# Routed experts in a two-layer trunk: expert rows summed in PSUM instead of stored and gathered, and slot rows read one block ahead on another queue

## The reference

```python
def moe_ffn(h, router_w, router_bias, w_gate, w_up, w_down):
    ...
    scores = jax.nn.sigmoid((t @ router_w).astype(jnp.float32))
    sel = scores + router_bias.astype(jnp.float32)
    ...                       # the best of 4 groups of experts, and in it the best 2 experts
    wsel = jnp.take_along_axis(scores, eidx, axis=-1)
    wsel = wsel / wsel.sum(-1, keepdims=True)
    comb = jnp.sum(jax.nn.one_hot(eidx, N_EXPERTS, dtype=jnp.float32) * wsel[..., None], axis=1)
    hg = jnp.einsum('td,edf->tef', t, w_gate)
    hu = jnp.einsum('td,edf->tef', t, w_up)
    act = jax.nn.silu(hg) * hu * comb[:, :, None].astype(t.dtype)
    return jnp.einsum('tef,efd->td', act, w_down).reshape(B, L, D)

# in trunk, for each layer:
        y = moe_ffn(h, ...)
        x = layer_norm(ALPHA * x + g2 * y, P['ln_w'][l, 1], P['ln_b'][l, 1])
```

## Time and profile before

| what | value |
|---|---|
| median of 3 runs | 1208.53 us |
| profiled execution | 1201.09 us |
| its span, and TensorE's mean granted clock | 1199.4 us, 0.951 |
| TensorE busy in the span | 1013.1 us (84%) |
| SyncE's queue q1 | 291.40 MB, 62.9% of 16 engines |
| POOL's queue q0 | 41.78 MB, 10.2% |
| ScalarE's queue q10 | 10.49 MB, 2.5% |

### The profile page before, as it was taken

One profiled execution on the slowest core, in us unless ns is written; L12 is line 12 of the kernel. 1 busy time (PEld: TensorE's weight loads), 2 busy tenths in 40 slices (PEclk: granted clock), 3 DMA queues, 4 the chain that ended last, 5 costly groups with the idle time before them and its releaser, 6 DMA issues.

```text
span 1199.4 us, 24149 instructions
## 1 busy us (share of the span) xinstructions
PE 1013.1 (84%) x9499; PEld 561.7 (47%) x9499; DVE 400.3 (33%) x1149; ACT 239.8 (20%) x507; POOL 190.9 (16%) x389
## 2 busy tenths in 40 slices
PE   4899998899769899795679999999978977998564
PEld 2344447654435455453345555455454544555231
DVE  0320115744612222121353533645552221222116
ACT  0401003631411121111131111210141121121102
POOL 0320000300032222122110001002004221222111
PEclk9999999899789999898889999999979998999988
DMA  8998232977589999999892314636765799899984
GB/s 354 324 343 299 95 126 97 350 298 317 222 302 396 388 407 393 397 399 394 305 377 99 140 71 143 243 123 241 292 256 211 270 391 408 337 395 393 394 349 158
DMA packets 76278, 344.62 MB, mean 287 GB/s; under 512 B 8883, under 2 KB 9011, under 8 KB 62900
## 3 DMA queue, kind: packets, MB, share of 16 engines
q1 hardware_dynamic: 54756, 291.40, 62.9%
q0 software_dynamic: 14512, 41.78, 10.2%
q10 hardware_dynamic: 6944, 10.49, 2.5%
HBM read 320.02 MB, written 23.63 MB: 287 GB/s over the span
## 4 chain that ended last, share of the span: by engine, by line
PE 63%; DMA 21%; DVE 10%; ACT 2%; issue 2%; SPq 1%; POOL 0%; POOLq 0%; ACTq 0%; DVEq 0%
PE bank L954 13%; PE bank L743 12%; PE bank L1019 11%; PE bank L961 7%; DMA ring<-in_moe_w_up_dram 7%; PE bank L872 7%; DMA ring<-in_ada_w_dram 3%; DMA ring<-in_moe_w_down_dram 3%; DMA arena<-in_moe_w_up_dram 3%; PE bank L633 3%; DMA ring<-in_ev_w_in_dram 3%; PE bank L1122 1%; PE bank L1098 1%; ACT arena L1409 1%; DVE arena L1531 1%
## 5 line engine op out<-in xcount | busy, mean ns | idle before, releaser
L954 PE MATMUL bank<-ring,arena 128*32 128x256 f32 x2496 | 149.9, 391 | 28.8 <-DMA ring<-in_moe_w_up_dram 25.7
L743 PE MATMUL bank<-ring,arena 128*128 128x512 f32 x336 | 146.7, 598 | 2.5 <-DMA ring<-in_ev_w_in_dram 2.5
L954 PE MATMUL bank<-arena 128*32 128x256 f32 x1792 | 108.1, 395 | 28.3 <-DMA arena<-in_moe_w_up_dram 28.3
L1019 PE MATMUL bank<-arena,ring 128*128 128x384 f32 x384 | 126.3, 492 | 1.9 <-issue 1.9
L1529 DVE TENSOR_TENSOR arena<-arena,bank 128x64 f32<-128x64 f32 x136 | 27.4, 201 | 296.2 <-ACT arena L1409 296.2
L954 PEld LDWEIGHTS bank<-ring,arena 128*32 128x32 f32 x2496 | 83.7, 113 | 88.5 <-issue 41.7
L961 PE MATMUL bank<-ring,arena 128*32 128x256 f32 x1440 | 87.0, 382 | 27.3 <-DVE arena L1531 22.2
L743 PEld LDWEIGHTS bank<-ring,arena 128*128 128x128 f32 x336 | 64.2, 192 | 82.9 <-issue 80.2
L1019 PEld LDWEIGHTS bank<-arena,ring 128*128 128x128 f32 x384 | 73.5, 192 | 54.4 <-issue 5.0
L954 PEld LDWEIGHTS bank<-arena 128*32 128x32 f32 x1792 | 60.3, 114 | 72.0 <-issue 39.4
L872 PE MATMUL bank<-ring,arena 128*128 128x512 f32 x192 | 83.2, 593 | 1.3 <-DVE arena L2096 1.3
(11 more groups left out here) (367 smaller groups left out, 1074.9 us busy)
## 6 DMA issues: line engine op xcount, KB each, us to landing
ring<-in_ada_w_dram SPq DMA_DIRECT2D x24, 2048.0 KB, 13.4
ring<-in_moe_w_down_dram SPq DMA_DIRECT2D x20, 2048.0 KB, 23.5
ring<-in_moe_w_gate_dram SPq DMA_DIRECT2D x18, 2048.0 KB, 24.1
ring<-in_moe_w_up_dram SPq DMA_DIRECT2D x18, 2048.0 KB, 29.4
arena<-in_moe_w_gate_dram SPq DMA_DIRECT2D x14, 2048.0 KB, 26.7
arena<-in_moe_w_up_dram SPq DMA_DIRECT2D x14, 2048.0 KB, 31.9
arena<-in_moe_w_down_dram SPq DMA_DIRECT2D x12, 2048.0 KB, 20.1
ring<-in_ev_w_in_dram SPq DMA_DIRECT2D x7, 2048.0 KB, 19.4
```

Source lines behind the costliest of these rows:

```text
L743: last = pe.matmul(bank[3 * (c % 2) + t], hT[:, k, t * P:(t + 1) * P], slot8(n)[:, k, :], start=k == 0, stop=k == KT - 1)
L954: last = pe.matmul(bank[1][q * BLK:(q + 1) * BLK, 0:HALF], slot_inT[:, k, :], both[:, :, k, q * P:(q + 1) * P], start=k == 0, stop=k == KT ...
L1019: last = pe.matmul(bank[c % 3][:, 0:T], slot8(n)[:, k, (c % 4) * P:(c % 4 + 1) * P], hT[:, k, :], start=k == 0, stop=k == KT - 1)
```

## The change

Expert results are no longer stored to DRAM and gathered. Six of the eight PSUM banks (`joined`) hold the sum for all 384 tokens over a whole expert stage. For each block VectorE builds a matrix `sel_w` that holds a token's routing weight where the token's slot lies in the block, and zero elsewhere; TensorE multiplies it with the block's result, 12 matmuls per block (`add_to_tokens`), each with 32 rows. They stand between gate and up of the next block and its down, and a last one behind the stage. In return the transposes on TensorE go (VectorE transposes the rows in blocks of 32), as do the gathers and the joins. Gate, up and down use banks 0 and 1 only.

The rows of a block are read by one DMA of 128 KB from ScalarE's queue into one buffer `slot_ahead`, in ScalarE's loop behind `row_rdy`; block 2's rows by SyncE. POOL only copies them. TensorE picks block 0 directly as channels by rows. The routing weights and slots of all tokens are spread to all partitions at the start of a stage (`along_tokens`). Behind layer 0 some column work is moved behind the first norms.

```diff
+        psum = ctx.enter_context(nc.psum_tensor("psum", [P, 8 * 512], F32))
+        bank = [psum[:, i * 512:(i + 1) * 512] for i in range(8)]
+
+        joined = psum[:, 2 * 512:8 * 512].rearrange("p (q t c) -> p t q c", q=4, t=NT)
...
-        slot_in = at(19456, 512, rows=2 * BLK)
+        slot_in = at(19456, 2 * P)
+        slot_ahead = at(19712, 2 * P)
         slot_inT = at(19968, KT, BLK)
         silu_g = at(20224, FT, BLK)
         act_rows = at(20352, FT, BLK)
         act_T = at(4096, FT, BLK)
-        slot_out = [at(4224, 512, rows=2 * BLK), at(6400, 512, rows=2 * BLK)]
-        slot_ahead = [at(5376, 512, rows=2 * BLK), at(5888, 512, rows=2 * BLK)]
+        slot_out = at(4224, HALF)
+        sel_w, sel_w1 = at(4736, T), at(5120, T)
+        token_slot, token_w = at(5632, 2, T), at(6400, 2, T)
         SPARE = 7168
-        picked = at(8192, NT, 2, D)
+        norm_scratch = at(8192, D)
...
+        def rows_in(queue, layer, block):
+            queue.dma_start(slot_ahead, slots[bass.ds(block * BLK, BLK), :].rearrange("s (g c) -> g s c", g=4)).then_inc(MS[layer]["row_in"], 16)
...
             blocks = pool.value_load(table[0:1, NE:NE + 1], min_val=NE, max_val=MAX_BLOCKS)
-            pool.wait_ge(trips_rdy, l + 1)
...
-
             before_last = pool.value_load(table[0:1, NE - 1:NE], min_val=NE - 1, max_val=MAX_BLOCKS)
-            pool.wait_ge(S["down_mm"], before_last)
-            pool.tensor_tensor(idle, wsel[:, 0, 0:1], wsel[:, 0, 0:1], ALU.add).then_inc(pool_chain, 1)
-            pool.wait_ge(pool_chain, 2 * l + 2)
+            with pool.Fori(2, blocks + 2) as b:
+                pool.wait_ge(S["row_in"], b * 16 - 16)
+                pool.wait_ge(S["rowT"], b)
+                pool.tensor_tensor(idle, eps_col, eps_col, ALU.add)
+                pool.tensor_copy(by_k(slot_in), slot_ahead.rearrange("p (s k) -> p k s", k=KT)).then_inc(S["row_rdy"], 1)
+
             if l == 0:
+                pool.wait_ge(S["row_rdy"], blocks + 1)
+                pool.wait_ge(S["down_mm"], before_last)
+                pool.tensor_tensor(idle, eps_col, eps_col, ALU.add).then_inc(pool_chain, 1)
+                pool.wait_ge(pool_chain, 2)
                 norm_gate_rows(pool)
-            for odd in range(2):
...
-                                            bass.IndirectOffsetOnAxis(ap=idx[:, r * NT + t:r * NT + t + 1], axis=0)).then_inc(gathered[t], 16)
+            pool.wait_ge(S["row_in"], blocks * 16 + 16)
+            pool.tensor_tensor(rows_over[:, l:l + 1], eps_col, eps_col, ALU.add)
...
-            for c in range(WARM):
-                pe.matmul(bank[3], ident, h_tok[:, c % NT, 0:512], start=True, stop=True)
-            rows_due = counter(pe, f"rows_due{l}", 1)
+
+            def along_tokens(b, column):
+                for t in range(NT):
+                    last = pe.matmul(b[:, t * P:(t + 1) * P], column(t).to_broadcast([P, P]), ident, start=True, stop=True)
+                return last
+
+            def begin_sums(b):
+                pe.matmul(b, tri[:, 0:1].to_broadcast([P, P]), keep[:, 0:512], start=True, stop=False)
+
+            pe.wait_ge(weights_rdy, l + 1)
+            for r in range(2):
+                last = along_tokens(bank[1 + r], lambda t: wsel[:, r, t:t + 1])
+            last.then_inc(spread_mm, 1)
+            for b in bank[3:]:
+                begin_sums(b)
+            pe.wait_ge(idx_rdy, l + 1)
+            pe.wait_ge(spread_act, 2 * l + 1)
+            for r, b in ((0, bank[1]), (1, bank[2])):
+                last = along_tokens(b, lambda t: slot_f[:, r * NT + t:r * NT + t + 1])
+            last.then_inc(spread_mm, 1)
             pe.wait_ge(table_rdy, l + 1)
             begin_of = EXPERT_ORDER + [NE]
             begin, end, after = 0, *[pe.value_load(table[0:1, begin_of[i]:begin_of[i] + 1], min_val=i, max_val=MAX_BLOCKS) for i in (1, 2)]
             pe.wait_ge(pick_rdy, l + 1)
+            for k in range(KT):
+                for t in range(NT):
+                    last = pe.matmul(bank[0][:, k * BLK:(k + 1) * BLK], h_tok[:, t, :].rearrange("p (c k) -> p k c", k=KT)[:, k, :],
+                                     pick[:, t, 0:BLK], start=t == 0, stop=t == NT - 1)
+            last.then_inc(pick_mm, 1)
+            pe.wait_ge(spread_act, 2 * l + 2)
             for t in range(NT):
-                for q in range(4):
-                    block, h = divmod(q, 2)
-                    last = pe.matmul(bank[2][q * BLK:(q + 1) * BLK, :], pick[:, t, block * BLK:(block + 1) * BLK],
-                                     h_tok[:, t, h * 512:(h + 1) * 512], start=t == 0, stop=t == NT - 1)
+                for g in range(4):
+                    last = pe.matmul(bank[1][g * BLK:(g + 1) * BLK, HALF:2 * HALF], pick[:, t, BLK:2 * BLK],
+                                     h_tok[:, t, g * HALF:(g + 1) * HALF], start=t == 0, stop=t == NT - 1)
             last.then_inc(pick_mm, 1)
-
...
-                last.then_inc(S["rowT_mm"], 1)
+            begin_sums(bank[2])
 
             def gate_and_up(s, k):
 
                 both = pair_of(s)
                 for q in range(4):
-                    last = pe.matmul(bank[1][q * BLK:(q + 1) * BLK, 0:HALF], slot_inT[:, k, :],
+                    last = pe.matmul(bank[0][q * BLK:(q + 1) * BLK, 0:HALF], slot_inT[:, k, :],
                                      both[:, :, k, q * P:(q + 1) * P], start=k == 0, stop=k == KT - 1)
                 return last
 
             def down(s, f):
 
-                for tile, q in enumerate((0, 2, 1, 3)):
-                    last = pe.matmul(bank[5][tile * BLK:(tile + 1) * BLK, 0:HALF], act_T[:, f, :],
+                for q in range(4):
+                    last = pe.matmul(bank[1][q * BLK:(q + 1) * BLK, 0:HALF], act_T[:, f, :],
                                      slot4(s + 2)[:, f, q * HALF:(q + 1) * HALF], start=f == 0, stop=f == FT - 1)
                 return last
 
+            def add_to_tokens(turn, closing=False):
+
+                for t in range(NT):
+                    if t == 2:
+                        pe.wait_ge(S["first_added"], turn)
+                        pe.sem_inc(passed, 1)
+                    for q in range(4):
+                        rows = slice(q * BLK, (q + 1) * BLK)
+                        half = NT * q + t
+                        last = pe.matmul(joined[:, t, q, :], sel_w[rows, t * P:(t + 1) * P], slot_out[rows, :], start=False,
+                                         stop=closing and t > (half ^ 1) % NT)
+                    if t == 0:
+                        last.then_inc(S["first_added"], 1)
+                return last
+
             def block_of_expert(b, s):
 
                 pe.wait_ge(S["rowT"], b + 1)
                 for k in range(KT):
+                    if k == KT - 1:
+                        pe.wait_ge(S["evac_dve"], b + 1)
+                        pe.wait_ge(S["evac_act"], b + 1)
+                        pe.wait_ge(S["sel"], b + 1)
                     last = gate_and_up(s, k)
                 last.then_inc(S["gu_mm"], 1)
-                rows_to_channels()
+                add_to_tokens(b + 1)
                 pe.wait_ge(S["act"], b * 2 + 1)
-                pe.wait_ge(S["evac_dve"], b + 1)
-                pe.wait_ge(S["evac_act"], b + 1)
                 pe.wait_ge(*full(s + 2))
                 down(s, 0)
                 down(s, 1)
...
                 down(s, 2)
                 down(s, 3).then_inc(S["down_mm"], 1)
 
-            pe.sem_inc(S["rowT_mm"], 1)
-            rows_to_channels()
             for i, place in enumerate(EXPERT_ORDER):
                 n = first + 3 * place
                 if i:
...
                     block_of_expert(b, n)
                 begin, end = end, after
             blocks = pe.value_load(table[0:1, NE:NE + 1], min_val=NE, max_val=MAX_BLOCKS)
-            pe.wait_ge(S["down_mm"], blocks)
...
-            pe.wait_ge(S["evac_act"], stores * 2 + 1)
+            pe.wait_ge(S["evac_dve"], blocks + 1)
+            pe.wait_ge(S["evac_act"], blocks + 1)
+            pe.wait_ge(S["sel"], blocks + 1)
+            pe.wait_ge(S["rowT"], blocks + 1)
+            pe.sem_inc(passed, 1)
+            add_to_tokens(blocks + 1, closing=True).then_inc(joined_mm, 1)
...
+            act.wait_ge(spread_mm, 2 * l + 1)
+            for r in range(2):
+                last = act.activation(token_w[:, r, :], bank[1 + r][:, 0:T], ACT.Copy)
+            last.then_inc(spread_act, 1)
+            act.wait_ge(spread_mm, 2 * l + 2)
+            for r, b in ((0, bank[1]), (1, bank[2])):
+                last = act.activation(token_slot[:, r, :], b[:, 0:T], ACT.Copy)
+            last.then_inc(spread_act, 1)
+            act.wait_ge(table_rdy, l + 1)
             act.sem_inc(S["evac_act"], 1)
-            pairs = act.value_load(trips[0:1, 1:2], min_val=NE // 2, max_val=MAX_BLOCKS // 2)
...
-            act.activation(warm, eps_col, ACT.Copy)
+            blocks = act.value_load(table[0:1, NE:NE + 1], min_val=NE, max_val=MAX_BLOCKS)
```

(54 more changed lines are left out.)

213 lines of the change are left out of this document (53 added, 160 removed).

## The result

The changed kernel takes 1464.47 us (median of 4 runs, 1458.96 to 1468.82), the kernel before 1209.87 us in the same comparison: a ratio of 1.212, 95% interval 1.208 to 1.216. It is slower by 255 us. The forecast was 1424 us in a range of 1250 to 1510.

The account below looks back on a forecast made before the run. Weight stream and TensorE were taken as nearly level in the expert stages. Stages +122 and +112, ends -18: +216 on the profiled 1201.1 gives 1417, with the median 7.4 higher 1424 us; range 1250 to 1510.

Parts of the forecast that it names:

- The slot rows: Expert stages: one row load under way, 4 engines with 32 packets each, 27 us beside weights, period 28, 150 us lost.
- 120 for the holds: Expert stages: blocks held by late row loads cost 120 us per layer.
- 17 for the clock: Expert stages: TensorE returns from holds at granted clock 0.50, some twelve bursts x 2.9, half hidden: 17 us per layer.
- The four fifths: Expert stages: of the 150 us lost per layer only four fifths, 120, was taken, for loads overlapping a burst's edges.
- The forecast's turn: Row loads beside weights: engines alternate one for one, a 16 KB weight packet and a 1 KB row packet, 0.65 us.
- The count of 219 against 214 packets: Earlier trace, x's load beside weights: queues move 219 and 214 packets in 6 us, taken as one for one.
- The block: TensorE's expert block: transposes go, twelve adds come at 1.5 us, period 6.32 becomes 6.8 (bounds 6.6 and 10.4).
- The first block: Start of both expert stages: block 0's pick 5.5 us, then 2.7 to the gate; about 3.3 us later.
- Behind the stages: After each expert stage: joins go, gate rows arrive late behind layer 0; gain 9 us each, 18 in all.
- Rival 1: Row load runs on all 16 engines: period 12.5, +63 and +53 per layer, 1306 us; chance 0.18.
- Rival 2: Engines serve a short row load in one go, about 7 us beside the stream, hardly any holds: 1175 us; chance 0.15.
- Rival 3: TensorE's adds run singly: 3.8 us more in each of 53 unheld blocks, over 1,600 us; chance 0.04.

Follow-up runs that it names:

- e7_two_buffers: Changed kernel with two buffers slot_ahead used in turn, so two row loads can be under way; same load shape and ScalarE queue: 1368.62 us, ratio 1.137.
- e2_pool_queue: Changed kernel with POOL instead of ScalarE issuing the row load right behind its copy, same shape and single buffer: 1355.37 us, ratio 1.125.
- e11_two_buffers_pool: Changed kernel with two buffers slot_ahead and POOL issuing the row loads, still one DMA of 128 KB per block: 1234.21 us, ratio 1.027.
- e3_small_weight_packets: Changed kernel with each expert matrix loaded by four DMAs of 512 KB in 4 KB packets instead of one in 16 KB packets: 1365.85 us, ratio 1.133.
- e6_contiguous_pick: Changed kernel with block 0's pick reading 128 neighbouring channels instead of every eighth (wrong channels for that block): 1452.47 us, ratio 1.203.
- e8_both_pool: Changed kernel with rows loaded by four DMAs on 16 engines, two buffers in turn, issued by POOL: 1200.55 us, ratio 0.995.

## Why the prediction was right, and where its sizes were off

**The slot rows.** Right in mechanism and nearly in size. Forecast: 4 engines, 32 packets each, 27 us beside the weights and 3.4 in calm, a period of 28 in the stream. Measured: 4 closing packets, 25 us and 4.1 with the issue, and periods of 26.0 (gate starts at 360.25 and 386.21) or 18 to 20. What I had pictured as one stream with 7 blocks in it is a row of bursts: a burst of four or more matrices holds a block for its load's full 25 us, a burst of three has 24 turns per engine, ends before the load's 32 are through and gives some 19 us. In layer 0 nine blocks are held, four by 19 us and five by 12, instead of seven by 21. The lost time, the slower clock in it, comes to 376.1 - 33 x 6.86 = 149.7 us in layer 0 and 374.9 - 34 x 6.86 = 141.7 in layer 1, where 120 for the holds and 17 for the clock were forecast, 137. The four fifths was a little too kind. That the sums are this near is in part luck: more blocks were held than counted, and each for less.

**How two queues share an engine.** The forecast's turn, one packet of each queue, is what the half microseconds show: three row packets in each, from four engines. The Trainium skill, DMA: Bandwidth & Descriptors, section Queues, rings and completion order, has an engine drain a packet of 9 to 17 descriptors from a ring before it turns. By that a load's 32 would go in two to four turns, and the weights would go in such turns too. The count of 219 against 214 packets, with which the prediction answered it, can't tell the two apart, as queues that take equal runs in turn also come out level; nor can the 25 us alone, since four turns behind the eight packets of a matrix (4 x 8 x 0.60 = 19 us) would last about as long. The half microseconds can, if the packets of the trace are its descriptors: a run of nine on one engine (0.05 us a packet) would show as nine at once. The measurement decides here.

**The block.** Period 6.86 for 6.8, adds 1.47 us between gate's end and down for 1.5: right. Taking them out shows that VectorE would need 0.93 us of the same time anyway.

**The first block.** Wrong in size: +3.3 forecast, +14.2 and +13.9 measured, half of the forecast's whole miss of 44 us. The step that failed is "48 records with 128-column weight loads (0.115 by the transposes' 0.46/4), 5.5 us". It took its price from weight loads of 64 rows with neighbouring elements. The same loads with neighbouring channels do take 5.67 us; with every eighth channel they take 11.52, 0.24 us per record, no more at half clock than at full. That is 6.0 of the 11 us missed in layer 0. Another 2.8 is a later start, which the forecast put at nothing: the pick begins at 330.52 and not at 327.76, in part because the matmuls that spread the slots over the partitions stand ahead of it (1.5 us). And the second pick and the opening of a bank take 4.5 us up to the gate, at half clock, and not 2.7.

**Behind the stages.** -7.3 and -9.6 for -9 and -9: right, and VectorE's first sum behind layer 0 waits 7.65 us for the gate rows, as forecast.

**The rivals.** Rival 1 (16 engines) was tried directly, and its mechanism holds with 1383 and not 1306 us. Rival 2 (no hold) is out: 1200 us is what a kernel without holds takes, with other loads. Rival 3 (adds one by one) is out.

**What the change itself is worth.** Summing in PSUM is sound. With loads that don't hold it, and block 0 picked as rows, it is 1.3% faster than before, which is about the 17 us that it saves behind the two stages. The loss came from how the rows are read, the shape of the load, its queue and its single buffer together (1200 us once all three are changed): a period of load + 1 us instead of two periods for a load. The strided pick costs another 11 us.

## What to carry to other kernels

Count the turns, not the bytes, of a small load that runs beside a large one: its time is the number of its packets per engine, closing ones included, times the packet times of both queues, and here some 5 us of issue and landing. Both factors can be changed (deal it on all 16 engines, or cut the other's packets). Give such a load two block periods by a second buffer (96 us in e7_two_buffers, some 120 between e2_pool_queue and e11_two_buffers_pool). Keeping a compute engine's queue free of waits that belong to a later block is argued from the held block, where this block's silu stood behind such a wait; no run shows its price apart. Price a strided weight load by a strided row, never by a contiguous one.

## What the runs showed of the hardware

- The same transfer, 128 KB from 32 rows of DRAM to 128 partitions, leaves 128 packets of 1 KB and 4 closing ones on ScalarE's queue, and 32 packets of 4 KB with 112 small ones on POOL's (e2_pool_queue).
- Where a row load ran beside the weights, the engines took one packet of each queue in turn: 3 row packets in each half microsecond on 4 engines, 32 turns in 20 us of a 25 us load beside 0.60 us weight packets, and in 7 of 12 us beside weight packets of 0.16 us (e3_small_weight_packets).
- TensorE's weight load of 128 columns took 0.24 us per record with a stride of 8 elements, no slower at granted clock 0.50 than at 1.00 (15 records in 3.5 us, 18 in 4), and 0.12 without the stride at 0.99 (e6_contiguous_pick).
- The weights needed 9% more engine time beside two row loads of 128 KB in 4 KB packets (e11_two_buffers_pool) than beside loads of 32 KB in 2 KB packets (e8_both_pool); 4 KB packets alone don't do it (40.5 us per MB in the kernel before), and the cause is open.
